# Mixture-of-experts stage of a decoder layer: results scattered to token rows, tokens gathered two experts ahead, experts in index order

## The reference

```python
def hierarchical_moe(x, w_group, b_group, w_router, b_router, w1, w3, w2):
    g_idx = argmax(x @ w_group + b_group)            # one of 8 groups
    e_logits = (x @ w_router + b_router)[group g_idx]  # its 8 experts
    top_vals, top_loc = top_k(e_logits, 2)
    weights = group_prob * softmax(top_vals)
    # for each chosen expert e of a token:
    #   y += weight * ((silu(x @ w1[e]) * (x @ w3[e])) @ w2[e])
```

```
experts  0- 7: 1 1 2 1 1 1 1 3     experts 32-39: 2 1 1 2 2 3 1 5
experts  8-15: 1 2 3 2 2 2 1 1     experts 40-47: 1 1 1 1 1 1 1 1
experts 16-23: 1 2 4 3 2 2 1 3     experts 48-55: 1 1 1 1 1 1 1 1
experts 24-31: 1 2 2 2 2 2 2 3     experts 56-63: 1 1 1 1 1 1 1 1
```

## Time and profile before

| | |
|---|---|
| median of three runs | 2192.16 us (2192.0 to 2193.31) |
| the profiled execution, its own time | 2188.43 us |
| its span in the profile | 2186.3 us |
| PE busy, DVE, ACT, POOL | 1819.5, 477.7, 252.1, 245.0 us |
| DMA | 510.97 MB, 461.36 of it on SP's queue |
| mean granted clock of PE | 0.924 |

### The profile page before, as it was taken

The page is one execution under the profiler, slowest core; times in us unless marked ns, Lnnn a source line. Parts: engine busy times, 40 slices in busy tenths (PEclk is TensorE's granted clock), DMA queues, the critical chain, the costliest instruction groups (busy, mean ns, idle before and its releaser), DMA issues.

```text
span 2186.3 us, 39333 instructions
## 1 busy us (share of the span) xinstructions
PE 1819.5 (83%) x13926; PEld 994.2 (45%) x13927; DVE 477.7 (22%) x1147; ACT 252.1 (12%) x543; POOL 245.0 (11%) x375
## 2 busy tenths in 40 slices
PE   7999999999999999999757567777777777676774
PEld 3676456644444444445534234444444444443442
DVE  5618214511110111146510000011011010001015
ACT  4012314200000000011100000000000000000002
POOL 1951000000000000001111011011111111111112
PEclk9999999999999999999779788899899888888898
DMA  6320321201111110073669999898999999999996
GB/s 194 145 61 22 128 77 34 68 2 43 43 43 43 43 43 38 0 288 122 250 265 419 419 413 401 346 406 339 407 401 403 405 401 410 408 399 407 410 365 237
DMA packets 152792, 510.97 MB, mean 234 GB/s; under 512 B 34400, under 2 KB 84064, under 8 KB 135840
## 3 DMA queue, kind: packets, MB, share of 16 engines
q1 hardware_dynamic: 122096, 461.36, 54.5%
q0 software_dynamic: 8816, 27.02, 3.5%
q10 hardware_dynamic: 21840, 22.06, 2.9%
HBM read 479.84 MB, written 34.35 MB: 235 GB/s over the span
## 4 chain that ended last, share of the span: by engine, by line
PE 59%; DMA 17%; ACTq 7%; SPq 5%; issue 4%; DVE 3%; ACT 2%; POOLq 0%; POOL 0%; DVEq 0%
PE act_bank L772 27%; PE dve_bank L772 15%; DMA unit_results<-lane_row 6%; PE act_bank L1114 5%; DMA unit_results<-spatialT 4%; ACTq L1328 4%; DMA gain_b<-xf_rows,gather_idx 4%; PE dve_bank L779 4%; PE act_bank L1100 3%; SPq L575 3%; SPq L520 2%; PE dve_bank L1114 2%; DMA tokens<-expert_token_table 1%; SPq L524 1%; ACTq L410 1%
## 5 line engine op out<-in xcount | busy, mean ns | idle before, releaser
L772 PE MATMUL act_bank<-norm_store,unit 128*128 128x512 f32 x1024 | 449.8, 592 | 0.2 <-DMA unit<-in_w_in 0.2
L772 PEld LDWEIGHTS act_bank<-norm_store,unit 128*128 128x128 f32 x1024 | 194.0, 190 | 239.4 <-issue 238.4
L1100 PE MATMUL act_bank<-unit,gain_a 128*32 128x256 f32 x3200 | 186.9, 385 | 24.5 <-issue 23.9
L1114 PE MATMUL act_bank<-unit,gain_a 128*32 128x256 f32 x2432 | 202.9, 490 | 0.0
L1846 DVE TENSOR_TENSOR gain_a<-gain_a,act_bank 128x128 f32<-128x128 f32 x100 | 28.8, 288 | 773.0 <-ACT gain_a L1321 765.0
L779 PE MATMUL dve_bank<-ident,gain_a 128*128 128x128 f32 x100 | 35.2, 352 | 169.2 <-DVE gain_a L1846 167.2
L1100 PEld LDWEIGHTS act_bank<-unit,gain_a 128*32 128x32 f32 x3200 | 109.3, 112 | 105.3 <-issue 49.8
L779 PE MATMUL dve_bank<-ident,gain_b 32*128 32x32 f32 x808 | 78.2, 242 | 77.4 <-DMA gain_b<-xf_rows,gather_idx 77.3
L1681 DVE TENSOR_TENSOR rows_store<-dve_bank,rows_store 128x512 f32<-128x512 f32 x48 | 33.3, 693 | 431.0 <-PE dve_bank L772 431.0
L1114 PEld LDWEIGHTS act_bank<-unit,gain_a 128*32 128x32 f32 x2432 | 95.1, 135 | 63.8 <-issue 42.5
L719 POOL DMA_INDIRECT gain_b<-xf_rows,gather_idx x101 | 94.3, 934 | 248.3 <-PE dve_bank L779 240.0
(11 more groups left out here) (268 smaller groups left out, 1507.8 us busy)
## 6 DMA issues: line engine op xcount, KB each, us to landing
unit<-in_w SPq DMA_DIRECT2D x112, 2048.0 KB
norm_store<-in_w SPq DMA_DIRECT2D x32, 2048.0 KB
mid_store<-in_w SPq DMA_DIRECT2D x32, 2048.0 KB
rows_store<-in_w SPq DMA_DIRECT2D x16, 2048.0 KB
unit<-in_w_gate SPq DMA_DIRECT2D x24, 512.0 KB, 5.2
unit<-in_w_in SPq DMA_DIRECT2D x4, 2048.0 KB, 8.7
unit_results<-unit POOLq DMA_DIRECT2D x4, 2048.0 KB, 13.4
unit_results<-lane_row ACTq DMA_DIRECT2D x200, 32.0 KB
```

What stands on the lines that cost most here:

```text
L772: ins = nc.tensor.matmul(out_, stationary, moving, start=first and n == 0, stop=n == len(pairs) - 1)
L1100: ins = nc.tensor.matmul(act_bank[0][h * CAP:(h + 1) * CAP, 0:2 * FQ].rearrange("t (w n) -> t w n", w=2), xT[:, k], w13[s][:, :, k, h * FQ ...
L1114: ins = nc.tensor.matmul(y_bank[s][z * CAP:(z + 1) * CAP, 0:DQ], hidT[:, j], w2s[s][:, j, z * DQ:(z + 1) * DQ], start=j == 0, stop=j == QU ...
```

## The change

Routing writes a different pair into the table for each choice: four times the token number, and a row of the results (each quarter of 256 columns is a row of its own). The table of row numbers is loaded four times per expert, once for each group of 32 partitions, and POOL adds the quarter's number. A gather then brings 128 rows of 256 values, quarter by quarter, and one DVE transpose makes `xT`; PE's eight transposes and DVE's copy are gone. An expert's first block (`open_rows`) and second (`next_rows`) are gathered two experts ahead; the third and later ones one block ahead. Each block of an expert also gathers the one two columns on, even where the list is over; such rows are out of range and are skipped.

ACT no longer stores results. POOL copies 128 row numbers into `y_idx` and scatters the tile to the rows of its tokens (`scatter`). So there are no rows to clear at the start, and at the end plain loads bring both results of a token. The lists are loaded by ACT, three experts ahead. The sorting and its two PE steps are gone: the experts run by index. The routing weights are laid out otherwise, so that the normed rows need no stride.

```diff
@@ each_unit
-                    if enter:
-                        enter(s, t)
+                    if enter:
+                        enter(s, t, first + shift)
                     with eng.Fori(first, end) as c:
...
-                        body(c, s, u, t, first)
+                        body(c, s, c + shift, t, first)
+                    if leave:
+                        leave(s, t, end, end + shift)
@@ SP
-            sp.wait_ge(rows_picked, 1)
+            sp.wait_ge(routed, 1)
             expert_up(up, 3, halves=(1,))
...
-                sp.dma_start(tokens[:, s], table_of[bass.ds(chosen_expert, 1)].rearrange("e p n -> (e p) n")
-                             ).then_inc(tokens_loaded[s], 16)
...
+            for s in range(SLOTS):
+                sp.wait_ge(per_slot["y_stored"][s], last[s] * 16 + 16)
             for i in range(NT):
...
+                sp.dma_start(y_both[i], y_tiles[i]).then_inc(row_loaded[i], 16)
@@ POOL
-            for z in range(2):
-                rows = (E + z * (UNITS - E) // 2) * CAP
-                for n in range(2):
-                    a = rows + n * 4 * P
-                    pool.dma_start(y_dram[a:a + 4 * P].rearrange("(p b) d -> p (b d)", p=P), unit[6][:, :]
-                                   ).then_inc(results_cleared, 16)
...
-            def gather(idx, u):
-                pool.wait_ge(tok_gathered, u * 16 + 16)
...
-                pool.wait_ge(tok_turned, u + 1)
...
+            def open_expert(s, t):
+
+                f = s % 2
+                pool.wait_ge(tokens_loaded[s], t * (16 * QUARTERS) + 16 * QUARTERS)
                 pool.nop(nofuse=True)
...
+                nc.gpsimd.tensor_scalar(tokens[:, s, 0:COLS], token_lists[:, s, 0:COLS], quarter_no[:, 0:1], None,
+                                        ALU.add).then_inc(list_made[f], 1)
+                pool.wait_ge(list_made[f], t * 2 + (s // 2 + 1))
...
+                gather(open_rows[f], tokens[:, s, 0, 0:1], open_landed[f])
+
+            def open_next(s):
+                gather(next_rows[s % 2], tokens[:, s, 1, 0:1], next_landed[s])
+
+            def scatter(c, s, first):
...
+                pool.wait_ge(per_slot["y_drained"][s], c + 2)
                 pool.nop(nofuse=True)
...
+                nc.gpsimd.tensor_copy(y_idx[:, s:s + 1], tokens[:, s, bass.ds(column, 1), 1]).then_inc(y_indexed[s], 1)
+                pool.wait_ge(y_indexed[s], c + 2)
+                pool.nop(nofuse=True)
+                pool.indirect_dma_start(y_dram, bass.IndirectOffsetOnAxis(ap=y_idx[:, s:s + 1], axis=0), y_rows[s],
+                                        None, bounds_check=2 * T * QUARTERS - 1, oob_is_err=False
+                                        ).then_inc(per_slot["y_stored"][s], 16)
+
+            def unit_work(c, s, u, t, first):
...
+                pool.wait_ge(xT_ready, turns_at(u, s, t) + 1)
...
+                gather(next_rows[f], next_idx[:, f:f + 1], next_landed[s])
+                scatter(c, s, first)
...
+            def enter(s, t, u):
+                pool.wait_ge(xT_ready, turns_at(u, s, t))
+                pool.nop(nofuse=True)
+                open_expert(*ahead(s, t))
+
+            def leave(s, t, end, units):
+                pool.wait_ge(next_landed[s], (end + t) * 16 + 16)
+                pool.nop(nofuse=True)
+                open_next(ahead(s, t)[0])
@@ ACT
-                for z in range(QUARTERS):
-                    act.dma_start(y_dram[bass.ds(u * CAP, CAP), z * DQ:(z + 1) * DQ],
-                                  y_rows[s][z * CAP:(z + 1) * CAP]).then_inc(per_slot["y_stored"][s], 16)
...
+            def list_ahead(s, t, u):
...
+                used = act.value_load(spans[0:1, 0, bass.ds(at, 1)], min_val=0, max_val=SLOT_UNITS)
+                chosen_expert = act.value_load(spans[0:1, 2, bass.ds(at, 1)], min_val=0, max_val=E - 1)
+                act.wait_ge(y_indexed[slot], used + 1)
+                load_list(slot, table_of[bass.ds(chosen_expert, 1)].rearrange("e p n -> (e p) n"))
@@ PE
-                turn_tokens(u + 1)
@@ DVE
+            def turn_tokens(rows):
+                v.transpose(xT, rows.rearrange("p (m k) -> p k m", k=KD)).then_inc(xT_ready, 1)
...
+            def unit_work(c, s, u, t, first):
+                gated(c, s)
+                dve.wait_ge(next_landed[s], (c + t) * 16 + 16)
+                turn_tokens(next_rows[s % 2])
+
+            def leave(s, t, end, units):
+                dve.wait_ge(xT_ready, turns_at(units, s, t))
+                dve.wait_ge(open_landed[(s + 1) % 2], t * (16 * 2) + 16 * ((s + 1) // 2 + 1))
+                turn_tokens(open_rows[(s + 1) % 2])
```

More of the change, by code:

```diff
@@ L291, in program @@
         x_loaded = [sem(f"x_loaded{s}") for s in range(2)]
-        x_root, x_row_loaded = sem("x_root"), [sem(f"x_row{i}_loaded") for i in range(NT)]
+        x_root, row_loaded = sem("x_root"), [sem(f"row{i}_loaded") for i in range(NT)]
         root_made = [sem(f"root_made{s}") for s in range(2)]
@@ new lines, in unit_work @@
+            def unit_work(c, s, u, t, first):
+                f = s % 2
+                column = nc.s_assert_within(c - first + 2, 0, COLS + 1, skip_runtime_bounds_check_because=(
+                    "an expert has at most T tokens"))
+                pool.wait_ge(xT_ready, turns_at(u, s, t) + 1)
+                pool.nop(nofuse=True)
+                nc.gpsimd.tensor_copy(next_idx[:, f:f + 1], tokens[:, s, bass.ds(column, 1), 0]
+                                      ).then_inc(next_indexed[s], 1)
+                pool.wait_ge(next_indexed[s], c + 1)
+                pool.nop(nofuse=True)
+                gather(next_rows[f], next_idx[:, f:f + 1], next_landed[s])
+                scatter(c, s, first)
@@ new lines, in ahead @@
+            def ahead(s, t):
+                return (s + AHEAD) % SLOTS, t + (s + AHEAD) // SLOTS
+            def enter(s, t, u):
+                pool.wait_ge(xT_ready, turns_at(u, s, t))
+                pool.nop(nofuse=True)
+                open_expert(*ahead(s, t))
+            def leave(s, t, end, units):
+                pool.wait_ge(next_landed[s], (end + t) * 16 + 16)
+                pool.nop(nofuse=True)
+                open_next(ahead(s, t)[0])
+            for s in range(AHEAD):
+                open_expert(s, 0)
+                open_next(s)
@@ L757, in _ @@
+            each_unit(pool, unit_work, enter, leave)
+            ends = [pool.value_load(spans[0:1, 0, E + s:E + s + 1], min_val=0, max_val=SLOT_UNITS) for s in range(AHEAD)]
+            for s in range(AHEAD):
+                pool.wait_ge(open_landed[s], 16 * (E // 2 + 1))
+                pool.wait_ge(next_landed[s], ends[s] * 16 + 16 * (TURNS + 1))
         @block.tensor
@@ L1804, in _ @@
-            v.tensor_scalar(placed, rev[0:E, :], place_col, None, ALU.is_equal).then_inc(order_known, 1)
-            n_at, first_at, end_at, shift_at, row_at0 = (in_order[:, n] for n in range(5))
-            n = job(dve_jobs, "order", 1)
-            dve.wait_ge(dve_filled, n + 1)
-            moved = dve_bank[n % 4][0:1, 0:3 * E].rearrange("p (n e) -> p n e", n=3)
-            step(v.tensor_copy(n_at, moved[:, 0]))
+            ts(n_at, n_at, ROUND, ALU.add)
+            ts(n_at, n_at, ROUND, ALU.subtract, 1.0, ALU.max)
```

318 lines of the change are left out of this document (125 added, 193 removed).

## The result

The changed kernel takes **2272.33 us** (median of four runs, 2270.03 to 2276.96), the kernel before in runs beside it 2192.08. The ratio is 1.037, 95% interval 1.035 to 1.039: slower by 80 us. The forecast was 2252, range 2150 to 2315.

What follows compares the result with a forecast made beforehand. The prediction took weight DMA to bound the kernel before, and ACT and POOL to bound experts 0 to 39 after. Stage +77, start -7 and tail -10 gave +60 on 2192.2 us: 2252 us, range 2150 to 2315.

Steps and rivals of the forecast that it cites:

- Start: Before the first gate matmul: shorter routing path, earlier half load and one DVE turn make it 7 us earlier (bounds 2 and 9).
- POOL's list: POOL's serial work per expert: 13.25 us with one block, including 2.9 us left of the wait in `leave`.
- 4.8 for each further block: POOL's time for each block after an expert's first: 4.8 us, giving POOL 703 us over experts 0 to 39.
- ACT's 721: ACT's time over experts 0 to 39: 40 x 9.2 us plus 36 further blocks x 9.8 us.
- the hand-over of 44: Experts 0 to 39: ACT and POOL hand lateness to each other, so 765 us was taken instead of 721.
- Order: Expert stage: index order puts 76 blocks in experts 0 to 39, taking 765 us; time lost there is not won back.
- Bytes: DMA queues: fewer stored rows and empty packets bring a light expert to 16.0 us (bounds 15.6 and 16.4).
- End: After the last result copy: 7.5 us to landed scatter, 21 of loads, 14 for the last tile; 10 us less.
- The signs: Expected profile: DMA share 0.8 to 0.9 over 39 experts, 3 us landing waits, copies 9 to 11 us apart, transpose near 0.42.
- (a): Rival: gather and scatter landings are short enough, so DMA bounds the stage; 2123 us, range 2120 to 2188, chance 0.23.
- (b): Rival: POOL's list is 17 us per expert and bounds light experts too; 2412 us, range 2310 to 2420, chance 0.11.
- (c): Rival: nothing changes, losses in the first part equal gains at start, tail and bytes; 2188 to 2205 us, chance 0.06.

Runs made afterwards that it cites:

- run 6: Changed kernel without the weight loads of experts 4 to 63 (results not the reference's): 2015.7 us.
- the fourth run: Changed kernel with four buffers for `next_rows` (one per slot) instead of two, and the old sorting put back: 2151.05 us, ratio 0.9805 to the kernel before.
- run 10: Changed kernel with SP's 2 MB half load also waiting for `list_made[0]`, so it goes out late, as in the kernel before: 2272.9 us.
- runs 6 and 7: Weight loads of experts 4 to 63 left out, in the changed kernel and in it with four `next_rows` buffers: 2015.7 and 2012.5 us.
- run 11: Changed kernel with four more register loads on POOL behind the wait in `leave`: 2368.35 us, ratio 1.082 to the kernel before.
- run 8: Changed kernel with four `next_rows` buffers, all scatter indices out of range so no result is stored, last loads reading w2 rows: 2162.66 us.
- run 3: Changed kernel in index order with four `next_rows` buffers instead of two, so the wait in `leave` is for an older gather: 2171.76 us, ratio 0.989.

## Why the prediction was right, and which steps were off

**The sum.** Forecast +60, measured +80 (spans +89.0). Stage: forecast +77, measured +101.8. Of the 25 us between, 22 lie in experts 0 to 39: 765 forecast, 787.4 measured. The light part was forecast at 336 and took 338.5. Start -7, measured -6.6; end -10, measured -6.2.

**POOL's list, the mis-sized term.** 13.25 us for a one-block expert stands: 13.5. Of its parts the wait in `leave` was larger, 142.2 us over 35 times, 4.1 each, not 2.9, and the others together smaller. The "4.8 for each further block" was the failing step. I added instructions and forgot that POOL's next body waits for DVE's turn, which comes once per block, and in an expert's last block too, where it turns rows of nobody and waits until they have landed. A further block took (793.6 - 40 x 13.5) / 36 = 7.0 us. With 7.0 in place of 4.8 the prediction's own formula gives 40 x 13.25 + 36 x 7.0 = 782 us, not 703, and 787.4 were measured.

It would be wrong to read these 7.0 as PE's 7.0. PE stood still for 79.9 us of the first part, 18 times, until DVE had turned, and DVE waited in 18 turns for the landing of a gather, 96.9 us. Without weights in the queues (run 6) DVE waits for no landing, and a further block takes (637.3 - 40 x 9.6) / 36 = 7.0 as well. Why the two agree stays open. A kernel that doesn't wait for the rows of nobody was not run.

**ACT's 721 and the hand-over of 44.** The forecast did not use POOL's 703 but took ACT's 721, the higher one, and added 44. ACT's 721 bounds nothing: with the wait in `leave` gone the first part takes 680 us. It costed a further block at 9.8 us by a landing of 8.1 for a scatter, where the trace of the changed kernel has a median of 6.3 over the first part; with four buffers a further block takes (682.5 - 40 x 9.9) / 36 = 8.0. One part of the 44 exists, the turn that waits for a gather issued one block before, but it was put at 12 us for experts of three blocks and more, and two-block experts have it too (the example above). So that 765 came near 787 is partly luck: 44 us of hand-over and a bound that doesn't hold stood in for 79 us missing in POOL's further blocks (36 x 2.2). The mechanism (a serial list on POOL with a landing inside) was right, and so was its place.

**Order.** I made one cause of order and list. They are two that add: 19 us for the order, 102 for the two buffers of `next_rows` with the wait in `leave`, and -41 for all the rest, as the fourth run against the kernel before shows. 2192 - 41 + 102 + 19 = 2272 (it closes because the runs differ by one step each).

**Bytes.** Forecast 16.0 us per light expert instead of 16.45. In the fourth run, where the weights are the bound in sorted order, they come at 214.83 MB in the 550 us from 1500 to 2050, which is 16.1 us per expert. That is 64 x 0.35 = 22 of the 29 us by which its stage is shorter (995 against 1024). The other 7 are a hole that is gone: the share from 1400 to 1450 is 1.02 in the fourth run, 0.88 before. In the first part of this kernel the term is hidden, since POOL's list is longer.

**Start.** From the last table scatter to the first matmul are 22.1 us before (from 1087.85) and 17.5 after. Step by step, before and after: scatter to list loads 4.9 and 5.3, list loads to gather 6.4 and 8.3, gather to turn 7.8 and 3.0, turn to matmul 3.0 and 0.8. So the gather did gain the 5 us of the forecast, but the lists ahead of it now pay some 4: with the load late (run 10) they are 4.5 us ahead of the gather and not 8.3. What is won for good is 2 us each by the shorter way from the lists to the gather and by the one turn in place of PE's eight and DVE's copy. The remaining 2 of the -7 are the earlier time of that scatter, as the forecast had it, but this time differs by up to 4 us between kernels that are the same up to it, so it shows nothing.

**End.** Last copy to first load 7.0 us (7.5 forecast), from there to the last multiply 25.8 (21 forecast), then 13.3 (14).

**The signs.** DMA share 0.86 in the first part: as said. Turn after some 760 us: about 790. Waits of 3 us, one per expert: 4.1. Copies of a slot 9 to 11 us apart: up to 15.9 (1572.59 and 1588.45, of which ACT waited 12.22 for the landing of the scatter). DVE's transpose at 0.42: it takes 0.64 (105.5 us over 165), and PE waits for it, twice in a row in the example above.

**Rivals.** (a) *Landings are short enough* is what happens without weights in the queues (runs 6 and 7: no wait left), and not with them. The Trainium skill, "DMA: Bandwidth & Descriptors", in its section on the anatomy of a SWDGE transfer, would give 2.3 us for 128 KB, an estimate. The run without weights does not contradict it (landed within about 3.1 us). The changed kernel does: its gathers from 1110 to 1740 landed after 2.2 us at least, 5.8 in the median and 7.8 at most. The prediction held ACT's stores of 8.8 us against that rule too, but the section is on DMAs that GpSimd issues, and those stores were not. (b) *POOL bounds everywhere*: not in the changed kernel, where the last twelve experts come every 15.5 us (2043.34 to 2229.26), with a DMA share of 1.02, as the weights do. With 2 us added (run 11) the list and the weights need about the same there. (c) fell.

## What to carry to other kernels

On an engine that serves a pipeline in order, a wait for one's own transfer is paid once per turn, less what the engine does in the meantime; cost it by the landing in full queues and give each slot its own buffer, if there is any room at all, so that the transfer waited for is an old one. When a list contains a wait for another engine, its cost per turn is not the sum of its instructions but at least that engine's period, and that engine may itself be waiting for a transfer of yours: look at what it waits for. A gather of no rows is waited for like any other. A delay put in to test a bound has to lengthen what the list is made of: here register loads did, and an arithmetic instruction vanished.

## What the runs showed of the hardware

- On POOL 1.04 us of tensor addition cost nothing beside indirect DMAs and register loads (gap ahead of the DMA 0.16 instead of 0.82 us, cycle of a one-block expert 13.5 in both), while four register loads cost 2.0 us (13.5 to 15.5).
- Gathers of 128 rows landed after 5.8 us in the median while 2 MB loads filled the queues, and within about 3.1 us without them; a gather of rows of nobody took 7.3 us in the example.
- A scatter whose rows are all out of range keeps ACT waiting about as long as a real one: longest 7.4 us in run 8 and in run 3, on the same tile. With all bytes of the scatters gone the kernel gained nothing clear of noise (ratios to the kernel before of 0.988 and 0.989).
- A 2 MB load issued just ahead of a small transfer went with a landing 4 to 5 us later (7.0 against 3.1 us for the lists, 7.9 against 3.0 for a gather), in the one place or in the other.
